# Experts fed by quarter rows that VectorE turns, with shaping and scaling on GpSimd

## What is computed

```python
x = layer_norm(alpha * x + g1 * y, ln1_g, ln1_b)
h = normalize(x) * (1 + sc2) + sh2          # modulate
p_g, grp = top_k(softmax(h @ w_rg + b_rg), 1)
p_e, local = top_k(softmax(logits_of_that_group), 2)
gate = p_g * p_e / sum(p_e)
# per token its two experts of 32, each a SwiGLU of width 512
y_e = (silu(h @ w_gate[e]) * (h @ w_up[e])) @ w_down[e]
x = layer_norm(alpha * x + g2 * sum(gate * y_e), ln2_g, ln2_b)
```

## Time and profile before

| | us |
|---|---|
| median of 3 runs | 1691.51 |
| lowest and highest run | 1689.35, 1691.93 |
| the profiled execution | 1683.64 |
| its span, first to last instruction | 1681.9 |
| `mixed_output` in it | about 998 to 1130 |
| `routing` | 1130 to 1157 |
| `experts` | 1157 to 1628 |
| `combine` | 1628 to 1682 |

### The profile page before, as it was taken

The page is one execution under the profiler, slowest core; times in us unless marked ns, Lnnn a source line. Parts: engine busy times, 40 slices in busy tenths (PEclk is TensorE's granted clock), DMA queues, the critical chain, the costliest instruction groups (busy, mean ns, idle before and its releaser), DMA issues. The chain is left out here.

```text
span 1681.9 us, 46845 instructions
## 1 busy us (share of the span) xinstructions
PE 1495.7 (89%) x19436; PEld 1102.2 (66%) x19436; DVE 927.6 (55%) x1855; ACT 694.2 (41%) x1585; POOL 209.9 (12%) x274
## 2 busy tenths in 40 slices
PE   5799998999977899986999989964999999998768
PEld 3578886779967788874666668852656565665433
DVE  6798762332115556558989957865151553444416
ACT  5444431012235455534767745532141433533311
POOL 0000001000034445324000000000000000000024
PEclk8899999999987999997999989985999999999989
DMA  9312324542133345213011024417849789999976
GB/s 369 114 63 95 100 79 161 201 157 76 50 108 116 109 116 142 85 54 122 20 44 51 7 92 176 163 67 287 350 166 379 268 333 418 414 420 418 370 259 242
DMA packets 115265, 305.31 MB, mean 182 GB/s; under 512 B 11010, under 2 KB 57682, under 8 KB 106074
## 3 DMA queue, kind: packets, MB, share of 16 engines
q1 hardware_dynamic: 93178, 244.95, 38.7%
q0 software_dynamic: 10336, 46.67, 7.8%
q10 hardware_dynamic: 11520, 10.49, 2.0%
HBM read 256.41 MB, written 45.67 MB: 180 GB/s over the span
## 5 line engine op out<-in xcount | busy, mean ns | idle before, releaser
L2753 PE MATMUL psum<-now_hidden,i_xm 128*32 128x256 f32 x4992 | 291.9, 387 | 13.0 <-DVE now_hidden L2863 12.2
L2753 PEld LDWEIGHTS psum<-now_hidden,i_xm 128*32 128x32 f32 x4992 | 162.1, 112 | 125.5 <-DVE now_hidden L2863 16.1
L2765 PE MATMUL psum<-now_down,i_hT 128*32 128x256 f32 x2464 | 147.1, 379 | 3.1 <-ACT now_down L2820 3.0
L2879 DVE TENSOR_TENSOR i_h<-i_silu,psum 128x128 f32<-128x128 f32 x78 | 22.2, 285 | 203.0 <-ACT i_silu L2813 203.0
L2863 DVE COPY now_hidden<-raw_hidden 128x1024 f32 x168 | 104.2, 691 | 27.1 <-DMA raw_hidden<-in_w_up 18.9
L2765 PEld LDWEIGHTS psum<-now_down,i_hT 128*32 128x32 f32 x2464 | 79.7, 110 | 57.2 <-ACT now_down L2820 5.0
L2803 ACT ACTIVATE i_xm<-psum,run_mod 128x128 f32<-128x128 f32 x163 | 63.2, 455 | 121.8 <-issue 81.8
L124 PE MATMUL psum<-hT_head,wm_head 128*128 128x512 f32 (+1 forms) x256 | 96.9, 378 | 11.2 <-DVE hT_rest L415 6.9
L1918 PE MATMUL psum<-dkT,f_qT 64*128 64x512 f32 (+1 forms) x384 | 89.7, 575 | 17.4 <-ACT f_E L1968 14.9
L1968 ACT ACTIVATE f_E<-psum,f_mx 128x1280 f32<-128x1280 f32 (+2 forms) x96 | 92.9, 972 | 18.6 <-DVE f_mx L2029 17.7
L124 PE MATMUL psum<-hT_head,wm_rest 128*128 128x512 f32 (+1 forms) x256 | 95.4, 373 | 0.0
(11 more groups left out here) (378 smaller groups left out, 3027.6 us busy)
## 6 DMA issues: line engine op xcount, KB each, us to landing
raw_hidden<-in_w_gate SPq DMA_DIRECT2D x22, 2048.0 KB, 24.9
raw_hidden<-in_w_up SPq DMA_DIRECT2D x22, 2048.0 KB, 30.4
raw_down<-in_w_down SPq DMA_DIRECT2D x22, 2048.0 KB, 21.1
wa_late<-in_w_ada POOLq DMA_DIRECT2D x16, 1024.0 KB, 5.6
yb<-i_y ACTq DMA_DIRECT2D x80, 128.0 KB, 10.0
wa<-in_w_ada SPq DMA_DIRECT2D x8, 1024.0 KB, 13.6
wt<-in_w_in SPq DMA_DIRECT2D x4, 2048.0 KB, 9.1
wm<-in_w_in SPq DMA_DIRECT2D x12, 512.0 KB, 4.0
```

The lines of the kernel that those rows point to most:

```text
L2753: last = nc.tensor.matmul(by_blocks(hidden_bank(s)[j * SUB:(j + 1) * SUB, :]), xm[u][:, k, s * SUB:(s + 1) * SUB], columns_of(now["hidden" ...
L2765: last = nc.tensor.matmul(down_bank(s)[j * SUB:(j + 1) * SUB, :], hT[s % 2][:, k * SUB:(k + 1) * SUB], now["down"][:, k, j * WIDE:(j + 1) ...
```

## The change

Eight things change together.

1. Rows are stored modulated. GpSimd, idle in `mixed_output` before, multiplies `xn` by 1 + scale and adds the shift (two operations of 128x1024 a row block, into `xs`), and SP stores `xs` as `xn2`. The two modulation rows are loaded to all partitions at the stage's start, 1 MB.
2. The unused quads: GpSimd makes a tile of zeros at the start of `mixed_output`, and SP stores it to all eight quads that may stay unused, two for each of the row blocks 1 to 4. The stores at the end of `experts` go.
3. `xn2` is seen as quarter rows of 256 values. The table `tok` is per block (96 columns) and partition: 4 x token + quarter, partition 32a + r holding quarter a of row r. TensorE makes it with 64 matmuls of 32 columns, four side by side, in float32 instead of 16 in the rounded form.
4. GpSimd gathers a block of 128 quarter rows of 1 KB into one of four buffers, four blocks ahead of the turn, instead of a quad of 4 KB rows.
5. VectorE turns a block in one transpose of 128x256 in 32x32 squares, read in steps of 8 elements (`turn_x`), behind `mix`, four blocks ahead, instead of TensorE.
6. ScalarE's shaping goes.
7. ScalarE takes the down result from PSUM (`keep_y`, behind `copy_down`), and GpSimd scales it with `rep_g` in SBUF (`scale`, behind the block's gather).
8. The stores of results wait for GpSimd's scaling; from quad 16 on ScalarE waits for it in each block.

```diff
+            for w in range(2):
+                sp.dma_start(late_mod[:, w, :], d["mod_rows"][3 + w:4 + w, :].to_broadcast([P, D])).then_inc(mod_loaded, 16)
...
+                if 1 <= t <= (QUADS - LOW) // 2:
+                    for q in range(LOW + 2 * (t - 1), LOW + 2 * t):
+                        sp.dma_start(ybq[q], nothing[:, :]).then_inc(nothing_stored, 16)
...
+            nc.gpsimd.memset(nothing[:, :], 0.0).then_inc(nothing_ready, 1)
+            pool.wait_ge(mod_loaded, 32)
+            nc.gpsimd.tensor_scalar(late_mod[:, 1, :], late_mod[:, 1, :], 1.0, None, ALU.add).then_inc(mod_ready, 1)
+            pool.wait_ge(mod_ready, 1)
+            for t in range(TL):
+                u = t % 2
+                pool.wait_ge(x_normed, t + 1)
+                if t >= 2:
+                    pool.wait_ge(xn_stored[u], 16 * (t // 2))
+                nc.gpsimd.tensor_tensor(xs[u][:, :], xn[u][:, :], late_mod[:, 1, :], ALU.mult).then_inc(x_scaled, 1)
+                pool.wait_ge(x_scaled, t + 1)
+                nc.gpsimd.tensor_tensor(xs[u][:, :], xs[u][:, :], late_mod[:, 0, :], ALU.add).then_inc(x_shaped, 1)
...
+        link(tt(is_row[:, :, :], each_pick(in_part[:, :], SUB),
+                small[:, COUNT:COUNT + SUB].unsqueeze(1).to_broadcast([P, PICKS, SUB]), ALU.is_equal))
         for j in range(2):
             here = slice(j * TL, (j + 1) * TL)
-            tt(part_hot[:, here, :], is_part[:, here, :], ids[:, :].unsqueeze(2).to_broadcast([P, TL, QUADS]), ALU.mult)
-            tt(row_hot[:, here, :], in_part[:, here].unsqueeze(2).to_broadcast([P, TL, P]),
-               small[:, COUNT:COUNT + P].unsqueeze(1).to_broadcast([P, TL, P]), ALU.is_equal).then_inc(picked, 1)
-
-        nc.vector.memset(tok[:, QUADS:], 0)
+            tt(row_hot[:, here, :], is_row[:, here, :], ids[:, :].unsqueeze(2).to_broadcast([P, TL, SUB]), ALU.mult)
+            tt(part_hot[:, here, :], part_of[:, here].unsqueeze(2).to_broadcast([P, TL, BLOCKS]),
+               small[:, COUNT:COUNT + BLOCKS].unsqueeze(1).to_broadcast([P, TL, BLOCKS]), ALU.is_equal).then_inc(picked, 1)
...
+        ts(tok[:, 0:BLOCKS], m.bank(2, BLOCKS), float(SUBS), small[:, QUARTER:QUARTER + 1], ALU.mult, ALU.add).then_inc(token_ready, 1)
...
+            for a in range(SUBS):
+                last = nc.tensor.matmul(m.bank(2, BLOCKS)[a * SUB:(a + 1) * SUB, :], row_hot[:, n, :], part_hot[:, n, :], start=(n == 0), stop=(n == PICKS - 1),
+                                        tile_position=(0, a * SUB))
...
-        def gather(q, i, u):
-            pool.wait_ge(x_turned[u], i)
-            pool.indirect_dma_start(out=xg[u][:, :], out_offset=None, in_=d["xn2"],
-                                    in_offset=bass.IndirectOffsetOnAxis(ap=tok[:, q:q + 1], axis=0)).then_inc(gathered[u], 16)
+        def gather(b):
+            pool.wait_ge(x_turned, b - RING + 1)
+            pool.indirect_dma_start(out=xg[b % RING][:, :], out_offset=None, in_=quarters(d["xn2"]),
+                                    in_offset=bass.IndirectOffsetOnAxis(ap=tok[:, b:b + 1], axis=0)).then_inc(gathered[b % RING], 16)
+
+        def scale(b, u, s):
+
+            pool.wait_ge(y_kept, b + 1)
+            nc.gpsimd.tensor_tensor(yo[u][:, s, :], yo[u][:, s, :], rep_g[:, :], ALU.mult).then_inc(y_scaled, 1)
+
+        def body(q, i, u, s):
+            b = q * SUBS + s
+            gather(b + AHEAD + RING)
+            scale(b, u, s)
 
         pool.wait_ge(routed, 1)
-        nc.gpsimd.memset(nothing[:, :], 0.0).then_inc(nothing_ready, 1)
-        blocks(pool, start=lambda q, i, u: gather(q + 2, i + 1, u))
+        pool.wait_ge(gate_loaded, 16 * SUBS)
+        for b in range(AHEAD):
+            gather(b + RING)
+        nb = blocks(pool, block=body)
...
-        def turn_x(i, u):
-            pe.wait_ge(gathered[u], 16 * i + 16)
-            pe.wait_ge(x_kept[1 - u], i + u)
-            for k in range(KD):
-                last = nc.tensor.transpose(m.bank(k // 4)[:, k % 4 * P:(k % 4 + 1) * P], run_columns(xg[u], k), ident)
-            last.then_inc(x_turned[u], 1)
...
+            pe.wait_ge(x_turned, b + 2)
...
+        def keep_y(b, i, u, s):
+            act.wait_ge(used["down"], b * KE + KE)
+            if s == 0:
+                act.wait_ge(stored[u], 16 * SUBS * i)
+            nc.scalar.activation(yo[u][:, s, :], down_bank(s), ACT.Copy).then_inc(y_kept, 1)
...
-                act.wait_ge(y_kept, b + 1)
+                act.wait_ge(y_scaled, b + 1)
...
+        def turn_x(b):
+
+            dve.wait_ge(gathered[b % RING], 16 * (b // RING) + 16)
+            if b >= RING:
+                dve.wait_ge(used["hidden"], (b - RING + 1) * KD)
+            nc.vector.transpose(xm[b % RING][:, :, :], run_columns(xg[b % RING])).then_inc(x_turned, 1)
...
-            keep_y(b, i, u, s)
+            turn_x(b + AHEAD)
...
+        turn_x(0)
...
+        turn_x(1)
         mix(0, 0)
+        for b in range(2, AHEAD):
+            turn_x(b)
```

More of the change, by code:

```diff
@@ L2091, in mixed_output @@
     w_route = m.sb("w_route", [P, KD, NG + NE])
+    nothing = m.sb("g_nothing", [P, D])
+    late_mod = m.sb("g_late_mod", [P, 2, D])
+    xs = [m.sb(f"g_xs{u}", [P, D]) for u in range(2)]
     m.top, m.limit = top, m.keep["outputs_at"]
```

123 lines of the change are left out of this document (46 added, 77 removed).

## The result

| | before | after |
|---|---|---|
| median of the runs compared | 1690.43 us | 1704.62 us (1701.83 to 1708.66) |
| ratio, 95% interval | | 1.0099, 1.0072 to 1.0125 |
| the profiled execution (its span) | 1683.64 (1681.9) | 1704.85 (1703.1) |
| `mixed_output`, first load of x to the gate's first load | 132.5 | 144.3 |
| from there to the start of the last down | 485.1 | 487.2 |

A forecast was written before the change was run, and what follows sets the result against it. In the experts TensorE bounds the first half, transfers the second; TensorE holds mixed output. Terms -12.0 + 5 + 0 + 2 + 0 + 0.8 - 1.2 - 1.3 = -6.7 us, from 1691.51 to 1684.8 us; range 1674 to 1698.

The forecast's parts named there:

- the seam: In the experts, the weight load issued at 1382.52 us: TensorE sets the pace ahead of it, transfers behind it.
- TensorE holds this stage: In mixed output, the claim that TensorE sets the time, being busy 12.00 of 12 us.
- Mixed output, +0.8: GpSimd's two operations fit a tile; +0.5 at the stage's end, +0.3 for modulation rows at its start; ends 0 and 2.5.
- The turns: In the experts, 10 turns of rows leave TensorE ahead of the seam, 1.2 us each: -12.0 us.
- VectorE's round: At a change of expert, VectorE's round grows from 6.15 to 7.1 us: +5 us, ends 0 and 16.
- gathers: In the experts behind the seam, gathering by quarter rows in 1 KB packets: +2 us, ends 0 and 7.
- last turn: In the experts, the turn on TensorE ahead of the last two blocks goes: -1.2 us.
- the start: Start of the experts: longer token table against smaller first gather and no first TensorE turn; 0, between -3 and +3 us.
- ScalarE: 0: In the experts, ScalarE loses two shapings a block, gains a copy, and its wait for GpSimd's scaling is covered: 0.
- that cover: In the experts, a hidden half of 3.4 us, beside which ScalarE's 2.05 us from quad 16 on would fit.
- End of the experts, -1.3: Without zero stores the last stores land earlier, the last result comes 0.7 us later: -1.3 us, ends 0 and -4.
- slower by VectorE's round: Rival, chance 0.20: both GpSimd operations stop expert weight copies for their whole length; sum +4.3 us, 1695.8 us.

The follow-up runs named there:

- GpSimd's order mended: The changed kernel with GpSimd scaling a block's result before it issues the next gather; 1698.47 us, ratio 1.0058 to the kernel before.
- the two operations alone: The kernel before plus only GpSimd's two operations per tile in mixed output, into buffers nobody reads; 1694.05 us, ratio 1.0045.
- late rows: The changed kernel with the modulation rows loaded behind the third tile's inputs instead of ahead of them; 1703.75 us, ratio 1.0093.
- the three runs with both corrections: Changed kernel, late rows, GpSimd's addition held back: VectorE scaling, ratio 0.9992; also zeros in tiles 4 to 7, 0.9974; that with GpSimd scaling before gathering, 0.9992.
- the one with zeros alone: The kernel before with only the zeroing of the unused quads moved into mixed output; 1688.76 us, ratio 1.0002.
- the two mended kernels: The changed kernel with GpSimd scaling ahead of the gather, ratio 1.0058, and the changed kernel with VectorE scaling results as before, ratio 1.0070.
- the version with both corrections: The changed kernel with late rows, GpSimd's addition held until VectorE's next norm is done, and results scaled by VectorE; 1684.45 us, ratio 0.9992.

## Why the prediction was wrong, step by step

**What bounds the kernel.** For the experts this held. With GpSimd's order mended the load at the seam stands 244.7 us after rep_g's load (1393.59), where it stood at 251.9 before and 252.7 after (1400.25), and the start of the last down moved by 6.0 of those 7.2. For `mixed_output` "TensorE holds this stage" rested on its being busy 12.00 of 12 us, and no pace was worked out. TensorE's transpositions of the heads, first two tiles of the kernel before and then two of the kernel after, give it:

```profile
1061.86 1.03 PE L1793 MATMUL psum<-mask,g_Y 128*128 128x128 f32 x8
...
1076.58 1.03 PE L1793 MATMUL psum<-mask,g_Y 128*128 128x128 f32 x8
...
1073.66 1.03 PE L1797 MATMUL psum<-mask,g_Y 128*128 128x128 f32 x8
...
1088.38 1.03 PE L1797 MATMUL psum<-mask,g_Y 128*128 128x128 f32 x8
```

That is 14.72 us a tile in both. VectorE's tiles had 14.23, half a us less, and have 14.87 after. So TensorE's pace in the middle of the stage did not change, and the margin that VectorE had under it is gone. (With the two operations alone TensorE's is 14.87 too: by this account it had no work left over from a slow stretch there, and followed VectorE.) The time is lost where TensorE waits for what VectorE and ScalarE make: early in the stage, and ahead of the last projection. With late rows those waits are 2.56 and 3.14 us; without GpSimd's second operation they are 0.67 and 0.25. Behind the longer one, at 1113.13 in that run:

```profile
1113.00:1117.00 4.00, 3.87 (x17) 3.84 (x18) 3.41 (x8) 1.17 (x3) 0.00 (x0) 0.53 0.32 131
1117.00:1121.00 4.00, 4.00 (x13) 3.08 (x12) 0.61 (x1) 0.54 (x2) 3.40 (x2) 0.62 0.00 0
```

By the granted clocks of 0.53 and 0.62, half speed lasted 6.8 of these 8 us, which costs TensorE 3.4 us of work; behind the first wait it is 1.7. An estimate from these figures: 4.8 us more of waits and 5.1 of low clock, less 1.2 by which TensorE's first turn of xn comes earlier in the stage, is 8.7, against 8.8 measured between the two runs. No run changed the clock alone.

**Mixed output, +0.8; measured +11.8, the largest error.** The step that failed is "GpSimd's two operations, 4.7 us, fit a tile". They fit in time, and still stood in the way of VectorE's product. The prediction had named this as a way to be wrong and given it no price, though the same 2079 ns were used for the experts. The runs split the 11.8: 3.0 for the modulation rows (forecast 0.3), 8.8 for the second operation. Told in VectorE's tiles, the second number is more than 7 at 0.64 us. The rest is the last tiles: in the runs with the collision the tile of the choice has a pitch of 18.2 to 18.6 us, without it 16.3 to 16.6, and the last 15.1 against 11.9 to 12.0, at the lower clock (the three runs with both corrections, without the collision, have 15.1, 13.5 and 13.5, and the one with zeros alone 12.7).

The Trainium skill (SBUF — State Buffer, "Who interferes with whom" and the rule on the shared pair above it) names exactly this case beside the copies: a `tensor_tensor` of VectorE with both inputs in SBUF contends with GpSimd's reads, and the loser waits for the whole instruction. The trace agrees for GpSimd's `tensor_tensor`: 1.31 us instead of 0.69, ending behind GpSimd's end at 1051.10. It does not for GpSimd's `tensor_scalar`, which reads SBUF too: with late rows the product at 1014.71 took 0.69 us in the midst of the one that runs for 2.79 us from 1013.47, and so it was in six more runs. The prediction weighed this rule for the copies of the experts only.

**The turns, VectorE's round, gathers, last turn: -12.0 + 5 + 2 - 1.2 = -6.2, with 0 for the start.** After, this stretch grew by 2.1 us instead (by 1.4 in the mean of four profiles each). With the scaling ahead of the gather it shrank by 6.0, with it on VectorE by 5.8. Of that, 1.7 to 2.0 came at the start, where the first hidden half begins 33.6 to 33.8 us after rep_g's load instead of 35.5, and 4.3 and 3.8 after it. So the net size came out for this stretch, but not each part. After, the round was 6.92 us against 7.1 forecast, the transpose 0.61 against 0.55: these were right. At 0.61 it is twice the 0.31 of the transpose of 128x128, which has half the elements, so the steps of 8 elements cost nothing that shows, and the 0.9 was not needed. In the two mended kernels the round is only 6.1 to 6.5, so by the forecast's own rule they should have gained some 3 to 4 us more than they did; part of it is in waits for now_down of 1.1 to 1.5 us in each of the first two runs of copy sets, part in the hidden half of the third block, which takes 4.56 and 5.91 us instead of 3.64, and the rest was not found. The step that failed is "ScalarE: 0". Its 2.05 us beside 3.4 us of cover counts the gather's own 1.05 but not the gather's wait for VectorE's turn, which stood behind a set of copies (6.12 us at 1254.65). Reversing two lines changed the stretch by 8.1 us, far more than the profiles of one code differ (0.7 us in the four of the change's experts, 1.4 and 2.2 in those of the two mended versions), so the order as the cause is shown; how the 8.1 divides between ScalarE's wait and the copies is an estimate. "If that cover is gone, a block pays the excess" was the right clause, and the wait ahead of the queued operation was not looked at.

**End of the experts, -1.3; measured +2.6.** The zeros are worth 0.7, not the whole of the term, and GpSimd's new presence to the end costs 1.8, which no step had. 2.6 + 0.7 - 1.8 leaves 1.5 of the 2.6 open, for ScalarE's and GpSimd's longer way of the last result (0.7 by the forecast) and for the last gathers.

**Sum and rivals.** -6.7, plus 11.0 in `mixed_output`, 8.1 for GpSimd's order and 3.9 at the end, is +16.3; the stages show +16.5. The rival "slower by VectorE's round" has the sign but not the cause: its round of 8.85 us did not come, since copies were stopped for the scaling (0.8 us a round) and hardly for the gather. The sign was decided outside the terms that had the widest ranges. The range was too narrow since three terms that were thought safe had upper ends of 2.5 (`mixed_output`), 0 (ScalarE) and 0 (the end).

## What to carry to other kernels

When work moves to GpSimd, set its operations against VectorE's order of operations, not against the stage's length; every `tensor_tensor` with both inputs in SBUF and every copy beside it is a candidate, and moving GpSimd's half into a stretch of statistics took 7.5 us back. On a queue in order, an operation that others wait for must stand ahead of one that itself waits for a slower engine: read what the issued gather waits for, not only how long it takes. An engine that is busy all the time in a loop has a pace; set beside it the pace of the engine that feeds it, for the difference is all that a longer operation there may take. Here it was 0.5 us a tile, and 0.64 came on top.

## What the runs showed of the hardware

- The exclusion: VectorE's 128x512 `tensor_tensor` from two SBUF tiles took 0.69 us alone and up to 1.48 beside GpSimd's multiplication or addition of 128x1024 (2.4 us); the one of 128x144 took 2.53 instead of 0.30, the one of 128x16 2.03 instead of 0.17. Beside GpSimd's `tensor_scalar` of 128x1024 (2.79 us) the 128x512 took 0.69, as alone. Statistics of 2 x 512 columns took 1.29 us beside the addition, as without. Copies of 128x1024 took at most 1719 ns beside gathers and scalings in the kernel after, at most 1251 with the scaling ahead of the gather, and at most 823 beside gathers alone (920 before).
- A gather's issue takes GpSimd 0.94 us at the least, up to 1.31 in the stage with copies beside them.
- TensorE's clock after a wait: waits of 1.89 us (1119.88), 1.21 us (1106.42) and 1.74 us (1038.35) were followed by 5 to 8 us at a granted clock of 0.50 to 0.63, in stretches in which other runs had 1.00, and 1.18 us by 0.63 over 4 us. Behind 0.28 and 0.73 us in the kernel before it stayed at 1.00, and so it did behind 1.20 us at 1263.39, in the middle of the experts, behind 1.40 us at 1032.23 in the version with both corrections, and behind 1.78 us at 1040.52 with the two operations alone. So the length of the wait does not tell it by itself. The same code in one stage took 133.8 or 137.4 us, by where TensorE waited and what the clock did behind it. An engine that gets ahead and then waits can thus end later than one that is never ahead.
- VectorE's turn of 128x256 in 32x32 squares, reading in steps of 8 elements, took 0.61 us; a turn of 128x128 took 0.31.
